# Expert layer of a streaming encoder: V rows by token, one block behind U, summed with 32-column weights

## The chip, the cores and the metric

The kernel runs on one core of one Trainium2 chip, in one launch. The metric is device time in microseconds (us), the median of three runs, from the first to the last instruction of the core. PE is the matrix engine, DVE the vector engine, ACT the scalar engine, POOL the engine that issues the indirect DMAs, SP the one that issues the plain ones.

## What is computed

One layer on 1024 prompt tokens, 32 sample tokens and 16 meta tokens of width 1024, all in fp32: a mixer (a projection, a gated linear recurrence beside a chunked matrix memory, an output projection) and then a layer of retrieved experts. The change touches the second.

```python
def block(xb):                                   # 128 tokens
    qh = (xb @ wq).reshape(PEER_BLOCK, PEER_HEADS, 2, PEER_HALF)
    s1 = jnp.einsum('thd,nd->thn', qh[:, :, 0], keys1).astype(jnp.float32)
    s2 = jnp.einsum('thd,nd->thn', qh[:, :, 1], keys2).astype(jnp.float32)
    v1, i1 = lax.top_k(s1, PEER_TOPK)
    v2, i2 = lax.top_k(s2, PEER_TOPK)
    cand = (v1[..., :, None] + v2[..., None, :]).reshape(PEER_BLOCK, PEER_HEADS, PEER_TOPK * PEER_TOPK)
    sc, ci = lax.top_k(cand, PEER_TOPK)
    e = (jnp.take_along_axis(i1, ci // PEER_TOPK, axis=-1) * PEER_KEYS
         + jnp.take_along_axis(i2, ci % PEER_TOPK, axis=-1))
    gate = jax.nn.softmax(sc, axis=-1)
    act = jax.nn.gelu(jnp.einsum('td,thkd->thk', xb, u_tab[e]).astype(jnp.float32)) * gate
    return jnp.einsum('thk,thkd->td', act.astype(xb.dtype), v_tab[e])
```

Each token picks 16 experts in each of 8 heads, 128 in all. An expert is one row of 1024 in u_tab and one in v_tab, both in HBM with 16384 rows each. The token's x is multiplied with its 128 U rows; the 128 results, through gelu and gate, weigh its 128 V rows. The sum is added to h, and a last norm gives y.

## The kernel before

The prompt is cut into 8 blocks of 128 tokens; the sample's 32 tokens are a block of their own ahead of them (b is None in the code), laid four times over the 128 partitions. The mixer of later tokens runs beside the experts of earlier ones: while block b's rows are gathered, the mixer works on block b + 1. Each engine has its program written out by hand in 128 ticks per block. In a tick, PE, DVE and ACT each do one expert's step and then what `beside` (L695, L944, L1299) puts there: the queries of a block at ticks 1 to 39 (head 0 already at tick 110 of the block before; `query` at L624, L887, L1086), the mixer at ticks 30 to 109 (`mixer` at L455, L762, L1111: projections at 37 to 78, the matrix memory from 74, the output projection at 91 to 103, the second norm at 105 to 109). All waits are counts of semaphores.

**Gathers.** The ring has eight buffers of 128 rows of 4 KB. POOL (`gathers`, L389, the DMA at L404) issues one indirect DMA per expert rank: partition p gets the row that token p has chosen as its e-th. Its order is alternating: U of tick t, V of rank t - 16; so the V rows of a head follow 16 ticks after its U rows, and the last 16 V of a block (`over`, L411) lie beside the first 16 U of the next. A gather waits until the buffer's last user is done: the dot of a U (s_dot) or the sum of a V (s_vsum). `row_of` (L241) gives the buffer and the count of arrivals. Per block: 128 U and 128 V gathers, plus 16 tiles of the query weights wq (512 KB each, two buffers) and x and y on SP's queue (`load_wq` L289, `load_x` L311, `store_y` L306).

**U side.** DVE multiplies the 128 rows with x (xcur, written by `take_over` on ACT, L910, once all dots of the last block are done) and sums along the row (`dot`, L1259; the instruction at L1266). After each head of 16, `gelu_arg` (L1268) and `coefficients` (L1281) make 16 coefficients per token, with an exponential on ACT (`gelu_exp`, L922) between them.

**V side.** ACT multiplies the identity with one coefficient column (`diagonal`, L926; all ACT instructions are recorded at L750) into one of four 128x128 buffers; PE multiplies that diagonal with the V rows, in two halves of 512 columns, and adds to acc in PSUM (`expert_sum`, L684; all matmuls are recorded at L428). A fp32 matmul is recorded as two. `take_up` (L672) first puts h into acc. At the end of a block ACT and DVE take acc out, norm it and SP stores y (`finish`, L935 and L1293). The first and the last part of the program, with fewer gathers beside the mixer, stand ahead of and behind the loops (L351, L419, L719, L977, L1336).

## Time and profile before

| what | value |
|---|---|
| median of 3 runs | 3569.66 us |
| lowest, highest run | 3557.79, 3579.22 us |
| profiled execution, first to last instruction | 3605.3 us |
| mean granted TensorE clock | 0.959 |
| instructions | 39214 |
| bytes moved | 1213.76 MB, mean 337 GB/s |
| busy: PE, DVE, ACT, POOL | 84%, 65%, 18%, 64% |

The profile gives no time of the profiled execution but its span. It is longer than each of the three timed runs, 1.0% above their median. Busy time of an engine is the union of its instructions. "Issue" as a reason for idle time means that nothing in the profile shows what was waited for. PEld is PE's weight load. The ends of matmuls are modelled, so distances between their starts are the safer reading.

### The profile page before, as it was taken

The page shows a single profiled execution, that of the slowest core. Times are in us where ns is not written, and L with a number is a line of the kernel's source. Part 1 is how long each engine was busy: PE and PEld are TensorE (multiplying, and loading weights), DVE is VectorE, ACT ScalarE, POOL GpSimd, SP SyncE. Part 2 cuts the span into 40 slices and gives each one's busy share as a digit, 9 for nine tenths or more (in the row PEclk, how much of TensorE's full clock was granted, in tenths as well). Part 3 has the DMA queues.
Part 4 walks back from the last instruction along what each step waited for, and adds up shares of the span by engine and source line. Part 5 has one row for each costly group of instructions (what it writes and reads, how often), then busy time and mean ns, then how long its engine had stood idle before and what let it go on. Part 6 is the DMA issues. An engine that isn't in the chain of part 4 may idle for free.

```text
span 3605.3 us, 39214 instructions
## 1 busy us (share of the span) xinstructions
PE 3011.3 (84%) x10724; PEld 1568.6 (44%) x10724; DVE 2354.0 (65%) x5813; ACT 658.5 (18%) x2015; POOL 2298.7 (64%) x2132
## 2 busy tenths in 40 slices
PE   7687888889987898879987798879987799877677
PEld 2553454345533454345533454345533454344222
DVE  3565975578656875578756876568655876568442
ACT  2211221112211221112211221112211121111111
POOL 0224666766777566766676567667676567667775
PEclk9799999989999999999999999999998999999999
DMA  6456989999999999999999999999999999999998
GB/s 241 161 174 240 366 316 346 371 354 351 337 372 378 348 338 351 348 361 359 330 368 357 363 314 355 361 340 369 341 353 355 364 327 345 350 375 373 355 368 296
DMA packets 340167, 1213.76 MB, mean 337 GB/s; under 512 B 41072, under 2 KB 41200, under 8 KB 339904
## 3 DMA queue, kind: packets, MB, share of 16 engines
q0 software_dynamic: 304128, 1107.43, 83.1%
q1 hardware_dynamic: 35776, 103.32, 7.7%
q8 instruction: 104, 1.70, 0.2%
q14 instruction: 159, 1.30, 0.1%
HBM read 1205.73 MB, written 4.87 MB: 336 GB/s over the span
## 4 chain that ended last, share of the span: by engine, by line
PE 37%; issue 20%; DMA 16%; DVE 9%; POOL 9%; another core or an unknown queue 6%; ACT 3%; POOLq 0%; ACTq 0%; SPq 0%; DVEq 0%
PE acc L428 23%; PE bank L428 13%; DMA ring<-peer_v,idx 11%; POOL ring L404 9%; DMA ring<-peer_u,idx 6%; DVE ring L1266 2%; ACT xn L750 1%; ACT diag L750 1%; DVE kw L1050 1%; DVE xn L1161 0%; DVE xn L1164 0%; ACT h L750 0%; ACT xT L750 0%; DVE topi L1052 0%
## 5 line engine op out<-in xcount | busy, mean ns | idle before, releaser
L428 PE MATMUL acc<-ring,diag 128*128 128x512 f32 (+1 forms) x4224 | 2086.7, 623 | 449.9 <-DMA ring<-peer_v,idx 269.1
L1266 DVE SCALAR_TENSOR_TENSOR ring<-ring,xcur 128x1024 f32<-128x1024 f32 x1056 | 1289.0, 1225 | 818.0 <-DMA ring<-peer_u,idx 744.5
L404 POOL DMA_INDIRECT ring<-peer_v,idx x1056 | 1151.2, 1090 | 643.6 <-issue 291.9
L404 POOL DMA_INDIRECT ring<-peer_u,idx x1056 | 1143.7, 1083 | 642.7 <-issue 316.5
L428 PEld LDWEIGHTS acc<-ring,diag 128*128 128x128 f32 (+1 forms) x4224 | 746.4, 192 | 1427.7 <-issue 1107.3
L750 ACT ACTIVATE diag<-ident,coef 128x128 f32<-128x128 f32 x1024 | 366.7, 395 | 646.7 <-PE acc L428 392.6
L428 PEld LDWEIGHTS bank<-xT,win 128*128 128x128 f32 (+1 forms) x2304 | 272.9, 183 | 79.2 <-issue 73.5
L428 PE MATMUL bank<-xT,win 128*128 128x128 f32 (+1 forms) x2304 | 282.6, 277 | 2.4 <-ACT xT L750 2.4
L750 ACT ACTIVATE G<-bank 128x128 f32<-128x128 f32 (+1 forms) x137 | 40.6, 296 | 830.4 <-PE bank L428 449.4
L428 PE MATMUL bank<-win,xT 128*128 128x512 f32 (+3 forms) x368 | 166.2, 583 | 1.9 <-ACT xT L750 1.9
L428 PEld LDWEIGHTS bank<-xT,qk 128*128 128x128 f32 x1024 | 131.5, 201 | 37.1 <-issue 37.1
L428 PEld LDWEIGHTS bank<-xT,t 128*128 128x128 f32 x1024 | 130.8, 200 | 36.2 <-issue 36.2
L428 PE MATMUL bank<-xT,qk 128*128 128x128 f32 x1024 | 131.3, 284 | 0.0
L428 PE MATMUL bank<-xT,t 128*128 128x128 f32 x1024 | 130.4, 283 | 0.0
L428 PEld LDWEIGHTS bank<-keysT,G 128*128 128x128 f32 x256 | 47.8, 200 | 132.9 <-issue 72.1
L428 PE MATMUL bank<-keysT,G 128*128 128x128 f32 x256 | 55.7, 301 | 57.5 <-ACT G L750 42.4
L428 PEld LDWEIGHTS bank<-win,xT 128*128 128x128 f32 (+2 forms) x368 | 60.3, 170 | 89.0 <-issue 88.7
L1266 DVE DVE_READ_ACCUMULATOR ring<-ring,xcur 128x1 f32 x1056 | 86.7, 82 | 0.0
L428 PE MATMUL bank<-wout,G 128*128 128x512 f32 (+1 forms) x144 | 70.5, 620 | 1.0 <-issue 1.0
L750 ACT ACTIVATE gl_a<-gl_a 128x16 f32<-128x16 f32 x66 | 14.0, 212 | 301.5 <-DVE gl_a L1275 154.3
L428 PE MATMUL bank<-wout,xc 128*128 128x512 f32 (+1 forms) x144 | 67.0, 593 | 0.0
L1049 DVE MAX8 tops<-bank 128x8 f32<-128x128 f32 x128 | 37.9, 296 | 31.3 <-PE bank L428 24.7
(227 smaller groups left out, 1821.1 us busy)
## 6 DMA issues: line engine op xcount, KB each, us to landing
qk<-wq SPq DMA_DIRECT2D x64, 512.0 KB
t<-wq SPq DMA_DIRECT2D x64, 512.0 KB
ring<-peer_u,idx POOLq DMA_INDIRECT x1056
ring<-peer_v,idx POOLq DMA_INDIRECT x1056
win<-w_in SPq DMA_DIRECT2D x6, 2048.0 KB, 15.1
ring<-wq SPq DMA_DIRECT2D x16, 512.0 KB, 5.1
wout<-w_out SPq DMA_DIRECT2D x1, 4096.0 KB, 22.8
xn<-x_prompt SPq DMA_DIRECT2D x8, 512.0 KB
```

The lines of the kernel that those rows point to most:

```text
L404: pool.indirect_dma_start(out=ring[:, slot, :], out_offset=None, in_=(peer_u, peer_v)[which], in_offset=bass.IndirectOffsetOnAxis(ap=idx[: ...
L428: return nc.tensor.matmul(out, lhsT, rhs, start=start, stop=stop)
L750: return nc.scalar.activation(out, in_, func, **kw)
L1049: link(dve.max(out_v[:, 0:8], values))
L1050: link(dve.match_replace(work, out_v[:, 0:8], values, -3.0e38))
L1266: stt(row, row, 1.0, xcur[:, :], ALU.mult, ALU.mult, accum_out=dots[:, column(b, e):column(b, e) + 1]).then_inc(s_dot, 1)
```

## The change

V rows are gathered by token: the partition is the expert slot (head and rank), and one DMA brings the 128 rows of one token. For that the index table is turned: DVE copies it to float, PE transposes it, ACT copies it out, DVE makes integers of it (`float_idx`, `turn_idx`, `turned_idx`). The coefficients are turned once per block by PE (`turn_coef`). A token's V sum is a matmul whose weights are 128 slots x 32 columns, all zero but one column, which holds the token's coefficients: a stripe wz with one filled column per 128 + 32, of which the matmul takes a window of 32 that puts the filled column at the token's place in its quadrant. The output is one of the four quadrants of 32 partitions of acc, and consecutive tokens go to different quadrants (`token_of`). ACT fills four tokens' columns in one copy (`token_weights`), in four sets.

The V rows of block b - 1 are gathered and summed beside the U rows of block b, eight ticks (LAG) behind. Block 0 has no V beside its U, and the V of block 7 come alone after its last U. The queries of a block begin eight ticks earlier, in `close` of the block before, where the last eight V gathers and sums lie. Gelu and coefficients are made in two groups of 64 ranks instead of eight of 16. The sum starts from a copy of h (hcur). The norm row of the second norm is no longer kept on all partitions: PE spreads it into PSUM per block. SP's stores of y move one block back. The sample keeps its scheme, with 32-column weights in wz.

```diff
 RING = 8
-DIAGS = 4
+SETS = 4
+GROUPS = 4
+LAG = 8
+HALF = 64
 QUERY_SLOTS = 5
...
-        ffn_bc = sb("ffn_bc", [P, D_MODEL])
+        ffn8 = sb("ffn8", [CM, P])
-        gl_a = sb("gl_a", [P, TOPK])
-        gl_b = sb("gl_b", [P, TOPK])
-        diag = sb("diag", [P, DIAGS, P])
+        gl_a = sb("gl_a", [P, HALF])
+        wz = sb("wz", [P, SETS * P + SAMPLE])
+        idxf = sb("idxf", [P, P])
+        idxv = sb("idxv", [P, P], u32)
+        coefT = sb("coefT", [P, P])
+        hcur = sb("hcur", [P, D_MODEL])
...
         def row_of(which, b, e):
-            turn, lead = 2 * P // RING, (2 * SAMPLE + TOPK) // RING
+            head, first, turn = 2 * SAMPLE - TOPK, (2 * SAMPLE + P) // RING, 2 * P // RING
             if b is None:
                 before, place = 0, 2 * e + TOPK + 1 if which else e if e < TOPK else 2 * e - TOPK
             elif which:
-                before, place = lead + b * turn, 2 * e + 1
-                if is_count(b, BLOCKS - 1) and e >= P - TOPK:
-                    place = e + P - TOPK
-            elif e >= TOPK:
-                before, place = lead + b * turn, 2 * e - 2 * TOPK
+                before, place = first + b * turn, 2 * e + LAG + 1 if e < P - LAG else e + P
+                if is_count(b, BLOCKS - 1):
+                    place = e
+            elif is_count(b, 0):
+                before, place = 0, head + (2 * e if e < TOPK else e + TOPK)
             else:
-                before, place = lead + (b - 1) * turn, 2 * (P - TOPK) + 2 * e
+                before, place = first + (b - 1) * turn, e if e < LAG else 2 * e - LAG
             return place % RING, (before + place // RING + 1) * 16
...
-            load_wq(0, range(10))
+            load_wq(0, range(12))
             store_y(None, y_sample)
-            with sp.Fori(0, BLOCKS - 1) as b:
+            load_x(1, x_prompt[P:2 * P, :])
+            load_wq(0, range(12, 16))
+            load_wq(1, range(10))
+            with sp.Fori(1, BLOCKS - 1) as b:
                 load_wq(b, range(10, 12))
                 load_x(b + 1, x_prompt[bass.ds(b * P + P, P), :])
                 load_wq(b, range(12, 16))
                 load_wq(b + 1, range(10))
-                store_y(b, y_prompt[bass.ds(b * P, P), :])
+                store_y(b - 1, y_prompt[bass.ds(b * P - P, P), :])
             load_wq(BLOCKS - 1, range(10, 16))
             store_states(1, BLOCKS + 1, BLOCKS)
-            store_y(BLOCKS - 1, y_prompt[(BLOCKS - 1) * P:BLOCKS * P, :])
+            for b in (BLOCKS - 2, BLOCKS - 1):
+                store_y(b, y_prompt[b * P:(b + 1) * P, :])
...
+                    if which == V and e == 0 and b is not None:
+                        pool.wait_ge(s_idxv, b + 1)
+                    if place >= RING:
+                        old, ob, oe = order[place - RING]
+                        pool.wait_ge((s_dot, s_vsum)[old], experts_before(ob) + oe + 1)
+                    elif held:
+                        for done, count in held[place]:
+                            pool.wait_ge(done, count)
+                            pool.sem_inc(s_pool_turn, 1)
                     if b is None and which == U and e == QUERY_SLOTS:
                         pool.wait_ge(s_sel, SAMPLE // TOPK)
                         pool.wait_ge(s_k_ps, 2)
                     pool.sem_inc(s_pool_turn, 1)
                     slot, _ = row_of(which, b, e)
+                    if which == V and b is not None:
+                        at = idxv[:, token_of(e):token_of(e) + 1]
+                    else:
+                        at = idx[:, column(b, e):column(b, e) + 1]
                     pool.indirect_dma_start(
                         out=ring[:, slot, :], out_offset=None, in_=(peer_u, peer_v)[which],
-                        in_offset=bass.IndirectOffsetOnAxis(ap=idx[:, column(b, e):column(b, e) + 1], axis=0)).then_inc(s_row[slot], 16)
+                        in_offset=bass.IndirectOffsetOnAxis(ap=at, axis=0)).then_inc(s_row[slot], 16)
...
-            def over(b):
-                last = (None, SAMPLE - TOPK) if is_count(b, 0) else (b - 1, P - TOPK)
-                return [x for t in range(TOPK) for x in ((U, b, t), (V, last[0], last[1] + t))]
+            def over():
+                return [x for t in range(TOPK) for x in ((U, 0, t), (V, None, SAMPLE - TOPK + t))]
+            def period(b, last):
+                both = [x for t in range(LAG, P) for x in ((U, b, t), (V, last, t - LAG))]
+                return [(U, b, t) for t in range(LAG)] + both + [(V, last, i) for i in range(P - LAG, P)]
+            def before_period(b):
+                return [((s_dot, b * P + (SAMPLE - RING + t + 1)), (s_vsum, b * P + (SAMPLE - P - LAG + t + 1))) for t in range(RING)]
             pool.wait_ge(s_qs_tile, 2 * PEER_HEADS)
             first = [(U, None, t) for t in range(TOPK)] + side_by_side(None, range(TOPK, SAMPLE))
-            gathers(first + over(0), None)
-            with pool.Fori(0, BLOCKS - 1) as b:
-                gathers(side_by_side(b, range(TOPK, P)) + over(b + 1), over(b)[-RING:])
+            gathers(first + over() + [(U, 0, t) for t in range(TOPK, P)], None)
+            with pool.Fori(1, BLOCKS - 1) as b:
+                gathers(period(b, b - 1), before_period(b))
             b = BLOCKS - 1
-            gathers(side_by_side(b, range(TOPK, P)) + [(V, b, j) for j in range(P - TOPK, P)], over(b)[-RING:])
+            gathers(period(b, b - 1) + [(V, b, i) for i in range(P)], before_period(b))
...
+                if tick == T_NORM2 + 1:
+                    if is_count(v, 0):
+                        pe.wait_ge(s_rows_bc, 32)
+                    pe.wait_ge(s_h2, w + 1)
+                    for c in range(CM):
+                        last = mm(by4(bank[c // 4])[0:n, c % 4, :], spread(ident[0:CM, c:c + 1], 1, n), ffn8[:, :])
+                    last.then_inc(s_ffn_ps, 1)
...
-            def expert_sum(b, j):
-                n = n_experts(b)
-                slot, arrived = row_of(1, b, j)
+            def sample_sum(j):
+                slot, arrived = row_of(1, None, j)
                 pe.wait_ge(s_row[slot], arrived)
-                pe.wait_ge(s_diag, experts_before(b) + j + 1)
+                pe.wait_ge(s_wz, j + 1)
                 for half in range(2):
-                    last = mm(acc[0:n, 512 * half:512 * half + 512], diag[:, j % DIAGS, 0:n],
-                              ring[:, slot, 512 * half:512 * half + 512], start=False, stop=j == n - 1)
+                    last = mm(acc[0:SAMPLE, 512 * half:512 * half + 512], wz[:, P * (j % SETS):P * (j % SETS) + SAMPLE],
+                              ring[:, slot, 512 * half:512 * half + 512], start=False, stop=j == SAMPLE - 1)
                 last.then_inc(s_vsum, 1)
-            def beside(b, tick, more):
+            def token_sum(b, i):
+                m, g = divmod(i, GROUPS)
+                slot, arrived = row_of(1, b, i)
+                if g == 0:
+                    pe.wait_ge(s_wz, sets_before(b) + m + 1)
+                pe.wait_ge(s_row[slot], arrived)
+                at = P * (m % SETS) + SAMPLE * (g + 1) - 1 - m
+                for half in range(2):
+                    last = mm(acc[SAMPLE * g:SAMPLE * g + SAMPLE, 512 * half:512 * half + 512], wz[:, at:at + SAMPLE],
+                              ring[:, slot, 512 * half:512 * half + 512], start=False, stop=m == P // GROUPS - 1)
+                last.then_inc(s_vsum, 1)
...
+            def close(b, last, more):
+                for k in range(LAG):
+                    if last is not None:
+                        token_sum(last, P - LAG + k)
+                    if more:
+                        queries(b + 1, k - LAG)
+                    if k == LAG - 2:
+                        turn_coef(b, more)
+                take_up(b)
...
+            def token_weights(b, m):
+                if m == 0 and is_count(b, 0):
+                    act.wait_ge(s_wz0, 1)
+                elif m == 0:
+                    act.wait_ge(s_ct, b + 1)
+                act.wait_ge(s_vsum, experts_before(b) + GROUPS * (m - SETS + 1))
+                to = wz[:, P * (m % SETS):P * (m % SETS) + P].rearrange("p (g c) -> p g c", g=GROUPS)[:, :, SAMPLE - 1]
+                a(to, coefT[:, :].rearrange("p (g m) -> p g m", g=GROUPS)[:, :, m], ACT.Copy).then_inc(s_wz, 1)
...
+                pe.wait_ge(s_coef, groups_before(b) + 2)
+                pe.wait_ge(s_topk, heads_before(b) + PEER_HEADS + (1 if more else 0))
+                nc.tensor.transpose(bB[:, 0:P], coef[:, :], ident[:, :]).then_inc(s_ct_ps, 1)
...
+            def close(b, last, more):
+                gelu_exp(b, 1)
+                if more:
+                    take_over(b + 1)
+                    for k in range(LAG):
+                        queries(b + 1, k - LAG)
+                turned_coef(b)
+                if last is not None:
+                    finish(last)
...
             def gelu_arg(b, g):
-                first = column(b, TOPK * g)
-                d = dots[:, first:first + TOPK]
-                dve.wait_ge(s_dot, experts_before(b) + TOPK * g + TOPK)
...
+                link(tt(c, d, gate[:, first:first + width], ALU.mult))
...
             def coefficients(b, g):
-                dve.wait_ge(s_gexp, heads_before(b) + g + 1)
-                link(ts(gl_a[:, :], gl_a[:, :], 1.0, None, ALU.add))
-                link(dve.reciprocal(gl_a[:, :], gl_a[:, :]))
-                tt(coef[:, column(b, TOPK * g):column(b, TOPK * g) + TOPK], gl_a[:, :], gl_b[:, :], ALU.mult).then_inc(s_coef, 1)
-            def dots_of(b, e):
-                dot(b, e)
+                width = TOPK if b is None else HALF
+                first = column(b, width * g)
+                c, x = coef[:, first:first + width], gl_a[:, 0:width]
+                dve.wait_ge(s_gexp, groups_before(b) + g + 1)
+                link(ts(x, x, 1.0, None, ALU.add))
+                link(dve.reciprocal(x, x))
+                tt(c, c, x, ALU.mult).then_inc(s_coef, 1)
...
+            def turned_idx(b):
+                dve.wait_ge(s_itf, b + 1)
+                if not is_count(b, 0):
+                    dve.wait_ge(s_vsum, experts_before(b))
+                dve.tensor_copy(idxv[:, :], idxf[:, :]).then_inc(s_idxv, 1)
...
+            def close(b, last, more):
+                gelu_arg(b, 1)
+                for k in range(LAG):
+                    if k == 1:
+                        coefficients(b, 1)
+                    if more:
+                        queries(b + 1, k - LAG)
+                if last is not None:
+                    finish(last)
+                turned_idx(b)
```

## Rows read from the trace of the kernel before

**Rows 1.** The page: busy shares of the engines, and the DMA digits by slice.

```profile
PE 3011.3 (84%) x10724; PEld 1568.6 (44%) x10724; DVE 2354.0 (65%) x5813; ACT 658.5 (18%) x2015; POOL 2298.7 (64%) x2132
...
DMA  6456989999999999999999999999999999999998
```

**Rows 2.** Stretches: from:to and length, busy us, clock, DMA share, GB/s.

```profile
1182.00:1592.00 410.00, 350.04 (x1252) 187.03 (x1252) 281.24 (x688) 76.14 (x235) 278.21 (x256) 0.97 0.95 351
...
3315.00:3565.00 250.00, 170.61 (x336) 58.53 (x336) 112.58 (x216) 32.95 (x88) 188.98 (x169) 0.98 0.96 354
1280.00:1400.00 120.00, 116.55 (x484) 67.16 (x483) 83.24 (x159) 23.83 (x72) 83.75 (x79) 1.00 0.94 339
1210.00:1250.00 40.00, 33.43 (x130) 18.98 (x131) 37.03 (x120) 9.69 (x30) 24.80 (x24) 0.96 1.02 406
...
3570.00:3588.00 18.00, 17.78 (x42) 7.90 (x42) 0.00 (x0) 4.90 (x14) 10.36 (x12) 1.00 0.98 366
```

**Rows 3.** Instruction groups of 1182:1592: busy us, mean ns | idle before, releasers.

```profile
L428 PE MATMUL acc<-ring,diag 128*128 128x512 f32 x512 | 251.2, 620 | 50.6 <-DMA ring<-peer_v,idx 31.6 <-ACT diag L750 13.5 <-issue 5.3
L1266 DVE SCALAR_TENSOR_TENSOR ring<-ring,xcur 128x1024 f32<-128x1024 f32 x128 | 156.4, 1225 | 94.5 <-DMA ring<-peer_u,idx 85.8 <-issue 7.3
L404 POOL DMA_INDIRECT ring<-peer_u,idx x128 | 141.0, 1102 | 52.3 <-issue 40.4 <-PE acc L428 10.4 <-DVE ring L1266 1.5
L404 POOL DMA_INDIRECT ring<-peer_v,idx x128 | 137.4, 1074 | 79.7 <-issue 33.4 <-PE acc L428 22.6 <-DVE ring L1266 12.0
...
L750 ACT ACTIVATE diag<-ident,coef 128x128 f32<-128x128 f32 x128 | 45.4, 395 | 63.8 <-PE acc L428 38.2 <-issue 17.5 <-remote 4.6
```

**Rows 4.** ACT's copies into xcur (start, us); dots: ns min/median/max, first and last start.

```profile
311.26 1.06 ACT L750 ACTIVATE xcur<-xn 128x1024 f32<-128x1024 f32 x1 [3.73 <-DVE ring L1266]
...
719.97 1.06 ACT L750 ACTIVATE xcur<-xn 128x1024 f32<-128x1024 f32 x1 [7.82 <-DVE ring L1266]
...
3178.72 1.06 ACT L750 ACTIVATE xcur<-xn 128x1024 f32<-128x1024 f32 x1 [8.33 <-issue]
...
L1266 DVE SCALAR_TENSOR_TENSOR ring<-ring,xcur x1056: 1160/1225/1300, 160.6 to 3566.7; 128x1024 f32<-128x1024 f32 x176
```

**Rows 5.** PE in order of time: start us, us; 32-column weights, then 128.

```profile
196.69 1.90 PE L428 MATMUL acc<-ring,diag 128*32 128x512 f32 x4
198.53 5.62 PE L428 MATMUL bank<-xT,win 128*128 128x128 f32 x48
...
1320.36 1.95 PE L428 MATMUL bank<-xT,win 128*128 128x128 f32 x16
1322.14 1.88 PE L428 MATMUL acc<-ring,diag 128*128 128x512 f32 x4
1323.86 0.38 PE L428 MATMUL bank<-xT,win 128*128 128x128 f32 x2
```

**Rows 6.** PE's records on acc in half us, sample queries: busy (x records).

```profile
110.00:110.50 0.50, 0.50 (x7) 1.00 0.89 229
110.50:111.00 0.50, 0.50 (x10) 1.00 0.83 344
...
111.50:112.00 0.50, 0.50 (x7) 1.00 0.88 336
```

**Rows 7.** One of the small gelu operations, whole run: busy us, mean ns.

```profile
L1273 DVE TENSOR_SCALAR gl_a<-gl_a 128x16 f32<-128x16 f32 x66 | 11.5, 175 | 2.3
```

**Rows 8.** The end, in order of time: PE, POOL, then ACT, DVE.

```profile
3570.42 27.70 PE L428 MATMUL acc<-ring,diag 128*128 128x512 f32 x64 [0.22 <-issue]
...
3571.56 0.94 POOL L404 DMA_INDIRECT ring<-peer_v,idx  x1 [0.30 <-issue]
...
3598.16 1.02 ACT L750 ACTIVATE xn<-acc 128x1024 f32<-128x1024 f32 x1 [6.46 <-PE acc L428]
...
3600.79 1.28 DVE L1297 SCALAR_TENSOR_TENSOR xn<-xn,stat,final_bc 128x1024 f32<-128x1024 f32 x1 [30.95 <-ACT stat L750]
```

**Rows 9.** One piece of the chain that ended last: start us, us, from issue to landing.

```profile
3317.33 5.33 DMA ring<-peer_v,idx
```

More of the change, by code:

```diff
@@ L52 @@
 T_QUERY0 = 110
+T_HCUR = 3
+T_IDXF, T_IDX = 60, 95
 T_MIXER = T_NORM
@@ L641, in query @@
                         pe.wait_ge(s_topk, heads_before(b) + head - 1)
+                    if ft == 5 and not is_count(b, 0):
+                        pe.wait_ge(s_ct, b)
                     pe.wait_ge(s_q2, b * 16 + ft + 1)
@@ L697, in beside @@
                 for head in range(1, PEER_HEADS):
                     query(b, head, tick - T_QUERY - QUERY_TICKS * (head - 1))
+            def beside(b, tick, more):
+                queries(b, tick)
                 if more:
@@ L701, in beside, with period @@
                     query(b + 1, 0, tick - T_QUERY0)
+                if tick == T_IDX:
+                    turn_idx(b)
+            def period(b, last, more):
+                for tick in range(P):
+                    if tick >= LAG:
+                        token_sum(last, tick - LAG)
+                    beside(b, tick, more)
+            def close(b, last, more):
[7 more added lines that the diff above has]
+                take_up(b)
             for tick in range(T_MIXER, BLOCK_TICKS):
@@ L942, in finish, with queries, beside @@
                 rstd(n, 6, D_MODEL).then_inc(s_rstd_y, 1)
-            def beside(b, tick, more):
+            def queries(b, tick):
                 for head in range(1, PEER_HEADS):
                     query(b, head, tick - T_QUERY - QUERY_TICKS * (head - 1))
+            def beside(b, tick, more):
+                queries(b, tick)
                 if more:
@@ L949, in beside, with period @@
                     query(b + 1, 0, tick - T_QUERY0)
+                if tick == HALF + 1:
+                    gelu_exp(b, 0)
+                if tick == T_IDX + 1:
+                    act.wait_ge(s_it_ps, b + 1)
+                    a(idxf[:, :], bF[:, 0:P], ACT.Copy).then_inc(s_itf, 1)
+            def period(b, last, more):
+                for tick in range(P):
+                    if tick % GROUPS == 2:
+                        token_weights(last, tick // GROUPS)
+                    if tick == T_HCUR:
+                        keep_h(b)
+                    beside(b, tick, more)
+            def close(b, last, more):
[7 more added lines that the diff above has]
+                    finish(last)
             nc.scalar.preload_act_table_set("natural_log_exp_and_others")
-            act.wait_ge(s_const, 7)
+            act.wait_ge(s_const, 6)
             act.wait_ge(s_setup_a, 1)
@@ L1287, in dots_of @@
-            def dots_of(b, e):
-                dot(b, e)
+                width = TOPK if b is None else HALF
+                heads = width // TOPK
+                first = column(b, width * g)
+                d, c, x = dots[:, first:first + width], coef[:, first:first + width], gl_a[:, 0:width]
+                dve.wait_ge(s_dot, experts_before(b) + width * (g + 1))
+                link(tt(x, d, d, ALU.mult))
+                link(ts(x, x, GELU_CUBIC, 1.0, ALU.mult, ALU.add))
+                link(tt(x, x, d, ALU.mult))
```

241 lines of the change are left out of this document (133 added, 108 removed).

## The prediction

> **What bounds the kernel now.** I began with the page [rows 1]: PE is busy 84% of the span, DVE 65%, POOL 64%, and the DMA digit stands at 8 or 9 from the fourth slice on. So I read next one period, the 410 us between two hand-overs of a block [rows 2] (1182:1592). It moves 351 GB/s at a DMA share of 0.95: 256 gathers of 128 rows of 4 KB (0.524 MB each), 16 tiles of wq and 1 MB of x and y. The 250 us in which nothing but gathers and sums ran [rows 2] (3315:3565) move 354 GB/s at 0.96 with PE at 68% and DVE at 45%. One gather per 0.524/354 = 1.48 us is thus what this ring of eight reaches without any crowd on the engines. With PE full, in the projections, it is 339 GB/s [rows 2] (1280:1400), and beside the query weights, which come by SP's queue, 406 GB/s in all [rows 2] (1210:1250).
>
> Then I asked who holds the gathers back. In the period POOL issues 256 of them in 278 us and sits idle 132 us more [rows 3]. About 0.30 us of idle stand between any two issues [rows 8], 77 us in all; the other 55 us are waits for a free slot of the ring, 33 us of them named after PE's sums and 13.5 after DVE's dots. PE waits 31.6 us for V rows and 13.5 us for ACT's diagonals; DVE waits 85.8 us for U rows [rows 3]. The gathers are the bound, first by their own rate, then by V slots that PE frees late.
>
> **The change, part by part.** Every number is set against the profiled span, 3605.3 us. That execution is 1.0% above the median of the three runs (3569.66 us); I carry the difference in us over to the median. Starting points: the hand-overs of x (the copy into xcur) are at 311.3, 720.0, ... 3178.7, so six and more periods of 409.6 us on average ((3178.7 - 311.3)/7), and the last dot ends at 3568, 389 us after the last hand-over and 37 us before the end [rows 4]. Up to 311 nothing of weight changes.
>
> *Block 0 without V.* The first period now gathers U alone, 128 gathers instead of 256. By gathers it would need 128 x 1.48 = 189 us and 16 tiles of wq. DVE doesn't let it: it is the engine with the most left to do. Its period is 410 us less the 85.8 us that it waits for U rows [rows 3] = 324. I take 8 off for the gelu (below) and add 2 for the index copies and the split multiplication by the norm row: 318 us, so -91 against 409. PE, which loses 251 us of sums in it, is out of the way. Lower end: DVE's waits for the other engines shrink too, 295. Upper end: the chains of the mixer, spread over 3.2 us ticks before, no longer fit under 2.4 us ticks, 340.
>
> *The V sums of a period.* A token still streams 2 halves of 512 columns in 4 records. A record takes 0.43 us with 128 columns of weights (1322.14 to 1323.86 are four) and no less with 32 (196.69 to 198.53: 1.84 us, 0.12 more) [rows 5]. Changing between the shapes costs PE time: the 48 projection records after it take 5.62 us where three runs of 16 at 1.78 (1320.36 to 1322.14) and a drain of 0.17 make 5.51 [rows 5]. So 0.12 + 0.11, I take 0.25 us per token beside which PE projects; some 65 ticks have such work: 16 us more of PE time in each period. Against it stands overlap. In the sample's queries the output quadrant changes every 32 records; just there ten records lie in half a us and otherwise seven [rows 6], so the new quadrant's records start while the old ones still stream. Consecutive tokens go to different quadrants. A token that finds PE behind, with its row landed and no projection between, can overlap the one before, up to 1.72 us. In a run of seven projection ticks three pairs stand together: in backlog 5.2 us saved against 1 us lost. [...]
>
> *Diagonals.* 128 ACT copies of 395 ns go, 45 us of ACT per period, and with them PE's 13.5 us of waiting for them [rows 3]; 32 strided copies of 4 columns, six ticks ahead, take their place. ACT was not the bound; only what PE frees earlier counts.
>
> *Gelu.* Eight groups of 11 small operations at about 0.2 us become two on 64 columns: 18 us to at most 6 us of DVE [rows 7], 12 less, 8 after the waits on ACT. Where DVE already waits for rows this gives nothing.
>
> *The close of a block.* After dot 127 DVE runs gelu, one and a half heads of queries, the last block's norm and the turned indices before its next dot: some 20 us. Meanwhile POOL has the last 8 V and 8 U of the next block, 16 x 1.48 = 24 us, then must wait for the turned indices and for dot 0. The queue runs dry for 3 to 6 us. The old crossing had its own wait of 8 us of POOL. I set the difference at 0, bounds -3 and +8.
>
> *Steady period.* Bounds: above 410, as now, and +8 for the close; below, 256 x 1.48 = 379 with no wait for slots at all, and wq in its shadow, which nothing in the trace does over a whole period; I put the end at 390 since DVE is at 93% in the query stretch [rows 2] (1210:1250). I take 402. The 120 us of projections going from 339 to 354 GB/s give 5 us, and of the 13.5 us for diagonals I count 3, as most of the rest is hidden in the same lateness. It is near the upper end because most V slots are late through projections, which stay. Six periods: -48. The last, without a mixer, -3.
>
> *The end.* Before, 37 us followed the last dot. Now: the last 8 V of block 6, 8 x 1.48 = 12; the sum of the last (2), ACT's two passes and the root (3600.79 - 3598.16 = 2.6), DVE's 1.28 and the copy of the indices (0.2) before the first V of block 7 may be issued; 5.3 us from issue to landing [rows 8, 9]: 24 us. Then 127 gathers of V alone. POOL's floor is 1.24 us each [rows 8], PE's 27.70/16 = 1.73 where sums don't overlap [rows 8]; the old V-only end ran at 366 GB/s, 1.43 us [rows 2] (3570:3588). I take 1.45 (overlap holds): 184. The last sum 2 and the finish 7: 217 in all, +180.
>
> Nothing else is on the path. The norm row by PE (8 small matmuls) runs beside ACT's square of the same 1024 columns, 1.02 us [rows 8]; ACT, 18% busy [rows 1], has room for the copy of h. SP stores y a block later and loads x behind that store as before, with most of a period to spare; if that cover failed, the mixer would start late by one transfer, some 5 us per block.
>
> Sum: -91 - 48 - 3 + 180 = +38. 3605 becomes 3643; the median 3569.66 becomes **3608 us**. Within this forecast the first period (295 to 340), the steady ones (398 to 406) and the tail (1.40 to 1.50) leave 3575 to 3645.
>
> **Rivals.**
> 1. *PE was the brake of the V slots and it is gone*: of the 55 us of slot waits a third goes, 18 us, every period takes 392, and block 0 takes 308. For it: most idle of POOL stands before V gathers (79.7 against 52.3) [rows 3]. Against it: the quiet 250 us reach only 354 GB/s. Six times -10 and -10, -10 for the seventh: -80 against my sum, 3528 us. Faster than before.
> 2. *The mode changes weigh more than the overlap*: in the mixed stretch no pair overlaps, 16 us of PE time go straight into the 200 us where PE is the bound, less 8 for the diagonals, periods of 418; and V alone runs at 1.73. Six times +16, and 127 x 0.28 = 36: +132, 3740 us. It decides from the point where the mean of PE's work per tick passes 2.9 us, the pace of two gathers.
> 3. *Periods stay at 410*: the change only moves work to both ends. 8 x 6 = 48 more, 3656 us. For it: the DMA share is 0.95 in crowded and in quiet stretches alike.
> 4. *V rows of one token come at another rate* than rows of one rank, since they share the first key; no row shows it. It would move the tail and the periods either way and lies inside 1 and 2.
>
> **Chances.** Forecast 40%, rival 1 20%, rival 2 13%, rival 3 27%. A measurement of this kernel tells some 0.5% (18 us) from no change. Faster: most of rival 1 and a sliver of mine, 0.20. Same: a third of mine and the edge of rival 1, 0.17. Slower: the rest, 0.63. The range runs from below rival 1 to above rival 3: 3510 to 3700 us, leaving out rival 2 and the tail of rival 1.
>
> **What would show it.** Hand-over 0 to 1 near 318 us with DVE over 85% busy and DMA near 0.65; later hand-overs 402 us apart; no wait of PE for ACT in the sums; about 9.5 us between sets of four V sums in quiet stretches and more than ten records in half a us where PE catches up; 190 us or less between the first and last sum of block 7, at 360 GB/s. Wrong if the steady periods differ from 402 by over 8, if block 0 takes under 295, or if the tail runs at PE's 1.73.

## The result, and the profile after

The changed kernel takes 3656.81 us (median of 5 runs, 3652.75 to 3675.40), against 3572.36 us for the kernel before beside it: ratio 1.025, 95% interval 1.0208 to 1.0292. A repeat beside the kernel before gave 3674.72 against 3566.56, ratio 1.0295 (1.0249 to 1.0342). Forecast was 3608, 1.1% slower or +38 us. Measured is +84 us between the medians: slower, as forecast, and inside the range of 3510 to 3700 us, but by more than twice as much.

The page of the changed kernel, where [rows 1] stand for the kernel before:

```profile
PE 2982.5 (81%) x10884; PEld 1214.2 (33%) x10884; DVE 2288.0 (62%) x5425; ACT 357.9 (10%) x1223; POOL 2297.6 (63%) x2131
...
PEclk9798777999999999999989999999999998999999
DMA  6456878999999998999999898999999998999898
```

The hand-overs of x in the changed kernel, in order of time (start us, us), against [rows 4]:

```profile
317.43 1.06 ACT L849 ACTIVATE xcur<-xn 128x1024 f32<-128x1024 f32 x1 [3.72 <-DVE ring L1407]
...
612.85 1.04 ACT L849 ACTIVATE xcur<-xn 128x1024 f32<-128x1024 f32 x1
...
3063.28 1.04 ACT L849 ACTIVATE xcur<-xn 128x1024 f32<-128x1024 f32 x1
```

Its dots (ns min/median/max, first and last start):

```profile
L1407 DVE SCALAR_TENSOR_TENSOR ring<-ring,xcur x1056: 1148/1224/1292, 164.4 to 3455.4; 128x1024 f32<-128x1024 f32 x176
```

These marks split the two profiled spans, 3605.3 and 3673.5 us:

| stretch | before | after | difference | forecast |
|---|---|---|---|---|
| start to hand-over 0 | 311.3 | 317.4 | +6 | 0 |
| block 0 | 408.7 | 295.4 | -113 | -91 |
| six periods (hand-over 1 to 7) | 2458.7 | 2450.4 | -8 | -48 |
| block 7, to its last dot's start | 388.0 | 392.1 | +4 | -3 |
| last dot's start to the end | 38.6 | 218.1 | +180 | +180 |
| sum | 3605.3 | 3673.5 | +68 | +38 |

The first row is scatter: in eleven other profiles of this kernel and its variants it lies between 311 and 318. Block 0 and the end came about as priced or better. The six periods hardly shrank: 408.4 us each, against 409.8 before and 402 forecast. Even these 8 us lie in the first of the six (395 us against 405); in the other five the periods are as long as before (411.1 against 410.8, from dot 127 to dot 127). The profiled executions are 68 us apart, the medians 84: 16 us of the slowdown stand in no row of this table.

The view of stretches (from:to and length, busy us of PE, PEld, DVE, ACT and POOL, granted clock, DMA share, GB/s) of the changed kernel: block 0; then one period cut at its dots 127, 40, 88, 127; then the V rows alone.

```profile
320.00:612.00 292.00, 164.44 (x820) 112.81 (x819) 267.59 (x634) 36.10 (x115) 181.45 (x146) 0.77 0.84 295
1415.70:1562.50 146.80, 116.88 (x447) 50.09 (x445) 112.56 (x339) 18.18 (x62) 89.07 (x83) 0.94 0.92 344
1562.50:1708.80 146.30, 138.65 (x573) 61.38 (x572) 100.95 (x182) 14.63 (x49) 105.80 (x98) 1.00 0.96 348
1708.80:1822.50 113.70, 94.55 (x252) 27.25 (x253) 60.08 (x119) 6.21 (x24) 80.78 (x78) 0.98 0.98 374
...
3480.00:3655.00 175.00, 169.10 (x483) 43.36 (x484) 0.00 (x0) 5.89 (x28) 113.16 (x122) 0.99 0.97 362
```

And the same three parts of a period of the kernel before:

```profile
1535.90:1675.80 139.90, 114.86 (x461) 66.72 (x462) 114.97 (x356) 29.09 (x94) 89.11 (x85) 0.96 0.97 367
1675.80:1825.70 149.90, 139.00 (x557) 78.54 (x555) 103.63 (x198) 29.13 (x87) 102.98 (x96) 0.99 0.93 334
1825.70:1941.20 115.50, 93.90 (x235) 40.41 (x236) 63.05 (x137) 18.12 (x53) 81.60 (x78) 0.97 0.98 370
```

In the first part, from the last dot of a block to dot 40 of the next, the DMA share fell from 0.97 to 0.92 and the rate from 367 to 344 GB/s; it is longer by 7 us in this period, 4.7 in the mean of five. In the second and third the rate rose and they are a little shorter (0.6 and 3.8 us in the mean). So about half of the gain forecast for the projections and the diagonals was there, nearly all of it behind the projections, and the crossing from block to block ate it. Where, DVE shows (start us, us, idle time before it in brackets; the small operations of gelu and of head 1's choices are left out):

```profile
1415.72 1.23 DVE L1407 SCALAR_TENSOR_TENSOR ring<-ring,xcur 128x1024 f32<-128x1024 f32 x1 [2.00 <-DMA ring<-peer_u,idx]
...
1425.79 0.30 DVE L1191 MAX8 tops<-bank 128x8 f32<-128x128 f32 x1 [5.93 <-PE bank L469]
...
1431.86 0.30 DVE L1191 MAX8 tops<-bank 128x8 f32<-128x128 f32 x1 [4.38 <-PE bank L469]
...
1440.13 1.28 DVE L1447 SCALAR_TENSOR_TENSOR xn<-xn,stat,final_bc 128x1024 f32<-128x1024 f32 x1 [3.46 <-ACT stat L849]
1441.34 0.22 DVE L1459 CAST idxv<-idxf 128x128 uint32<-128x128 f32 x1
1446.06 1.23 DVE L1407 SCALAR_TENSOR_TENSOR ring<-ring,xcur 128x1024 f32<-128x1024 f32 x1 [4.50 <-issue]
```

Thirty us between two dots: two waits for head 1's scores, one for the norm, and 4.50 us in which the profile shows nothing, at the turn of DVE's loop over blocks. POOL in the same place:

```profile
1438.37 0.94 POOL L437 DMA_INDIRECT ring<-peer_u,idx  x1 [1.43 <-issue]
1448.10 1.09 POOL L437 DMA_INDIRECT ring<-peer_u,idx  x1 [8.79 <-DVE ring L1407]
1450.90 0.94 POOL L437 DMA_INDIRECT ring<-peer_v,idxv  x1 [1.72 <-DVE ring L1407]
1453.51 0.94 POOL L437 DMA_INDIRECT ring<-peer_u,idx  x1 [1.67 <-DVE ring L1407]
1456.37 0.94 POOL L437 DMA_INDIRECT ring<-peer_v,idxv  x1 [1.93 <-DVE ring L1407]
...
1471.52 0.94 POOL L437 DMA_INDIRECT ring<-peer_u,idx  x1 [2.02 <-DVE ring L1407]
```

The ring (the eight buffers that all gathers share) holds eight U rows and nothing else. The wait of 8.79 us was expected in kind. What was not: each of the next eight gathers, U or V, waits for one dot, and a dot beside a choice comes only every 2.9 us. These eight gathers take 23.4 us (1448.10 to 1471.52), where the queue at 1.48 us each would need 12.

### The profile page after: what moved, and what is told of

It is laid out like the page before. It is cut to its first block, busy times and chain, and to the rows that moved or that the text cites. A ratio compares the mean times of both kernels' runs of the same rounds, so it can differ in the third digit from the quotient of the medians.

```text
span 3673.5 us, 37305 instructions
## 1 busy us (share of the span) xinstructions
PE 2982.5 (81%) x10884; PEld 1214.2 (33%) x10884; DVE 2288.0 (62%) x5425; ACT 357.9 (10%) x1223; POOL 2297.6 (63%) x2131
## 4 chain that ended last, share of the span: by engine, by line
PE 32%; issue 20%; DVE 18%; DMA 16%; POOL 8%; another core or an unknown queue 3%; ACT 1%; POOLq 0%; DVEq 0%; SPq 0%; ACTq 0%
PE acc L469 20%; DMA ring<-peer_v,idxv 13%; PE bank L469 12%; POOL ring L437 8%; DVE ring L1407 6%; DMA ring<-peer_u,idx 3%; DVE kw L1192 1%; DVE kw L1202 1%; DVE eh L1203 1%; DVE kw L1200 1%; DVE topi L1194 1%; ACT xn L849 1%; DVE tops L1193 1%; DVE topi L1195 1%
## 5 line engine op out<-in xcount | busy, mean ns | idle before, releaser
L469 PE MATMUL acc<-ring,wz 128*32 128x512 f32 x4224 | 1892.2, 617 | 386.7 <-DMA ring<-peer_v,idxv 341.9
L437 POOL DMA_INDIRECT ring<-peer_u,idx x1056 | 1125.6, 1066 | 781.8 <-issue 448.6
L437 POOL DMA_INDIRECT ring<-peer_v,idxv x1024 | 1135.0, 1108 | 544.9 <-issue 281.0
L469 PEld LDWEIGHTS acc<-ring,wz 128*32 128x32 f32 x4224 | 376.9, 111 | 1577.8 <-issue 871.3
L469 PE MATMUL bank<-xT,win 128*128 128x128 f32 (+1 forms) x2304 | 292.7, 283 | 5.8 <-issue 3.3
L469 PE MATMUL bank<-xT,qk 128*128 128x128 f32 x1024 | 142.9, 297 | 22.8 <-DMA qk<-wq 20.7
L469 PE MATMUL bank<-xT,t 128*128 128x128 f32 x1024 | 141.3, 295 | 23.8 <-issue 19.2
L1447 DVE SCALAR_TENSOR_TENSOR xn<-xn,stat,final_bc 128x1024 f32<-128x1024 f32 (+1 forms) x9 | 11.6, 1284 | 231.3 <-ACT stat L849 229.0
L469 PE MATMUL bank<-keysT,G 128*128 128x128 f32 x256 | 66.3, 343 | 92.4 <-ACT G L849 84.7
L849 ACT ACTIVATE wz<-coefT 128x4 f32<-128x4 f32 x256 | 49.7, 206 | 470.7 <-PE acc L469 293.1
```

What stands on the lines that cost most here:

```text
L437: pool.indirect_dma_start(out=ring[:, slot, :], out_offset=None, in_=(peer_u, peer_v)[which], in_offset=bass.IndirectOffsetOnAxis(ap=at, a ...
L469: return nc.tensor.matmul(out, lhsT, rhs, start=start, stop=stop)
L849: return nc.scalar.activation(out, in_, func, **kw)
```

## Experiments

For every kernel the starts of its 1024 prompt dots were taken from the trace and averaged over blocks 2 to 6 (the first column is from dot 127 of the block before to dot 0; "V alone" is the time from first to last gather of block 7's V, over 127):

```
                         127-0   0-8  8-40  40-88 88-127  period  V alone
before                     3.2  26.8 112.4  150.6  117.8   410.8     -
after                     30.1  23.4  93.5  150.0  114.0   411.1   1.438
after, repeated           30.3  23.4  92.9  151.3  112.8   410.7   1.438
e1 late close             22.3  28.6  93.4  152.3  115.4   412.1
e2 queries at tick 1      24.2  15.8  97.6  148.2  113.3   399.2
e10 queries at tick -3    27.5  22.3  94.1  150.2  112.9   406.9
e9 e2 and late close      14.8  21.8 100.9  147.5  113.5   398.5   1.426
e3 same quadrant          31.4  23.4  93.5  154.6  113.2   416.2   1.640
e8 wide weights           30.1  23.4  93.1  150.6  114.3   411.5   1.679
e4 rows of a rank         29.9  23.4  93.8  152.2  112.7   412.0   1.444
e5 half sums              28.8  23.4  94.0  147.3  114.1   407.7   1.398
e7 half sums and dots     32.1  19.2  91.5  149.9  112.5   405.3   1.403
e11 e9 without loops      14.2  20.3 100.4  146.6  114.0   395.5
e12 before without loops   3.5  26.4 105.5  150.8  115.7   401.8
```

Two executions of the changed kernel differ by up to 1.3 us in a column. e3, e4, e5, e7, e8, e2 and e10 were timed once each.

**e1, the close itself.** In DVE's program:

```diff
+                if more:
+                    period(b + 1, True, range(DOTS_FIRST))
+                turned_idx(b)
                 if last is not None:
                     finish(last)
-                turned_idx(b)
```

and the loop starts at tick 2 (DOTS_FIRST is 2).

> From the changed kernel, where dot 0 of a block starts 30.1 us after dot 127 of the block before (mean of blocks 2 to 6) and a period takes 411.1 us. Here DVE does dots 0 and 1 of the next block, and turns the indices, before the last norm, and takes its loop turn (4.5 us without an instruction) behind them. Theory A (the close eats the gain: POOL waits for dot 0 with a dry queue): dot 0 comes 21 to 24 us after dot 127, the period is 403 to 407 us, and the whole kernel 30 to 55 us faster than the changed one. Rival B (the gathers' own rate sets the period, and what is lost in the close is made up later): dot 0 is earlier as well, but the period stays within 2 us of 411 and the whole within 12 us.

Dot 0 came 7.8 us earlier, as expected, but ranks 0 to 8 took 5.2 us more, since the loop turn and the norm now lie there, and the period is 412.1. 3668.83 us (ratio to before 1.0174, 1.0115 to 1.0232), 5 us under e4, whose stretches are the changed kernel's, on the same chip. These are rival B's numbers. Theory A falls in this form: moving the gap doesn't remove it.

**e2, the queries back at tick 1.**

```diff
-T_QUERY = 1 - LAG
+T_QUERY = 1
...
                 if last is not None:
+                    act.wait_ge(s_xcur, streams_before(b) + (2 if more else 1))
                     finish(last)
```

> The queries begin at tick 1 again, so that the close holds none of head 1's choices. Theory A: the stretch without dots falls from 30 to 20 us or less, but the queries then reach 8 ticks further into the block, where DVE is 93% busy; ranks 0 to 40 take 7 to 10 us more than 117, so that the period is 408 to 413 us. Theory C (the earlier queries are themselves the loss): the period falls to 404 us or less. Rival B: 411 within 2 us.

3597.27 us in one run, 76.6 under e4 (one run too) on the same chip; before stood at 3612.30 there (3582.27 to 3617.69). The period is 399.2: theory C's number. The edit is the tick and a wait of ACT for its own copy of x. The stretch without dots shrank by only 6 us, though; ranks 0 to 8 gave 7.6, and ranks 8 to 40, where the moved choices now lie, took back 4.1. DVE's busy time from dot 127 to dot 40 is the same (112.4 against 112.6 us, means of the same blocks). POOL of e2 at the crossing:

```profile
1422.22 0.94 POOL L437 DMA_INDIRECT ring<-peer_u,idx  x1 [0.30 <-issue]
1430.12 1.14 POOL L437 DMA_INDIRECT ring<-peer_u,idx  x1 [6.95 <-DVE ring L1408]
1431.56 1.99 POOL L437 DMA_INDIRECT ring<-peer_v,idxv  x1 [0.30 <-issue]
1433.86 1.99 POOL L437 DMA_INDIRECT ring<-peer_u,idx  x1 [0.30 <-issue]
1436.15 0.94 POOL L437 DMA_INDIRECT ring<-peer_v,idxv  x1 [0.30 <-issue]
...
1445.91 1.08 POOL L437 DMA_INDIRECT ring<-peer_u,idx  x1 [2.76 <-PE acc L469]
```

DVE finds eight landed U rows and no choice to make beside the first ones; its dots run back to back, and behind the same kind of wait (6.95 us) eight gathers take 15.8 us (1430.12 to 1445.91) instead of 23.4. Its first part of a period, against 0.92 and 344 GB/s above:

```profile
1401.90:1541.60 139.70, 115.18 (x457) 50.98 (x456) 112.52 (x339) 18.51 (x62) 92.63 (x85) 0.99 0.95 363
```

That made theory D: what costs is the stretch from dot 127 to dot 8, in which only dots free slots.

**e10, queries at tick -3.**

```diff
-T_QUERY = 1 - LAG
+T_QUERY = -3
```

ACT's wait is in it as in e2. It tells D from the wait inside the close: here no choice of DVE lies in the close, but seven lie beside dots 0 to 7.

> Queries from tick -3: PE and ACT still have part of head 1's work in the close, but DVE's first choice of head 1 falls beside dot 1, so seven choice steps lie beside dots 0 to 7, against eight in the changed kernel and three or four in e2. Theory D (a dot beside a choice takes 2.9 us and frees one slot, so ranks 0 to 8 are slow by the number of choices beside them): ranks 0 to 8 take 21 to 23 us, the period is 404 to 409 us. Rival C (it is the wait of DVE inside the close, for scores that PE makes between V sums): the period falls to e2's 399 or below, since no choice is left there.

22.3 us and a period of 406.9; 3633.72 us in one run. Both as D says, and C as this expectation puts it (the wait inside the close is all of it), 399 or below, falls. The wait has a part, though: of the 4.2 us that the period lost, 2.6 are in the stretch without dots and 1.1 in ranks 0 to 8. Between ticks -7, -3 and 1 the period goes 411, 407, 399.

**e9, both edits.** e2, and in DVE's close:

```diff
+                if more:
+                    period(b + 1, True, range(1))
+                turned_idx(b)
+                if more:
+                    period(b + 1, True, range(1, DOTS_FIRST))
                 if last is not None:
                     finish(last)
-                turned_idx(b)
```

(DOTS_FIRST is 3.)

> Queries from tick 1 (as e2) and, in DVE's order, dot 0 of the next block, then the turned indices, dots 1 and 2, and only then the last norm and the loop turn. Theory D (what costs is the stretch from dot 127 to dot 8, in which eight lone U rows fill the ring and only dots free slots; it took 53.5 us for 21.4 gathers in the changed kernel and 40.0 for 21 in e2): dot 0 comes at 16 to 19 us, dot 8 at 31 to 36 us after dot 127, the period is 391 to 396 us against e2's 399.2, and the whole kernel 30 to 50 us below e2's 3597, thus 1 to 3% below the kernel before. Rival B (the gathers' own rate, 1.47 us, makes up for whatever the close loses): within 3 us of 399.

Dots 0 and 8 came at 14.8 and 36.6 us, nearly as D expected, but ranks 8 to 40 took 3.3 us more than e2's, and the period, 398.5, is rival B's: the second edit brought nothing that these runs can tell (e2's one run was 0.996 of the kernel before on its own chip). From dot 127 to dot 40 the DMA share is now that of the kernel before:

```profile
1398.00:1535.40 137.40, 114.12 (x453) 51.73 (x452) 113.00 (x340) 18.52 (x62) 89.29 (x84) 0.96 0.97 369
```

84 gathers and the wq tiles fill it. 3571.45 us in 10 runs, 103 under the changed kernel beside it (3674.72), and 1.0005 (0.9982 to 1.0028) of the kernel before: the slowdown is gone, and no more.

**e3 and e8, overlap and shape changes.** e3 gives consecutive tokens to one quadrant (its sums and `token_weights` take their places from i accordingly); e8 uses all 128 columns of a set as weights and writes all of acc, so that neither quadrants nor shape changes are left. First e3's edit, then e8's:

```diff
-            return SAMPLE * (i % GROUPS) + i // GROUPS
+            return i
```

```diff
-                    last = mm(acc[SAMPLE * g:SAMPLE * g + SAMPLE, 512 * half:512 * half + 512], wz[:, at:at + SAMPLE],
+                    last = mm(acc[:, 512 * half:512 * half + 512], wz[:, at:at + P],
```

> Consecutive tokens go to the same quadrant of 32 partitions, so their matmuls can't overlap; the four columns of a set lie in one block of coefT. If the overlap is what kept PE out of the way: the 128 gathers of V alone at the end go from 1.44 to about 1.7 us each (+35 us), and ranks 40 to 88, beside the projections, from 150 to 156 to 160 us. If the gathers' rate hides PE (rival B): the end still becomes slower since 1.73 us of PE per sum is over 1.44, but ranks 40 to 88 stay within 2 us of 150. If matmuls of different quadrants don't overlap in these sums at all: nothing changes, 1.44 and 150.

> From the changed kernel; the V sums use 128 columns of weights and write 128 partitions, as before the change (each row is then added with four tokens' coefficients: that part of the output is another computation). Neither shape changes nor overlap are left. e3 (no overlap, shape changes) took 5.5 us more per period and 1.64 us per gather of V alone. If the shape change costs 0.25 us at each of some 65 ticks and PE were the bound there, this gives back up to 8 us of e3's loss beside the projections: ranks 40 to 88 at 147 to 151 us, V alone at 1.62 to 1.73 us. If the gathers hide the shape changes: ranks 40 to 88 at 153 to 156, as e3.

e3 took 3738.21 us and e8 3718.93, one run each on different chips. Without overlap ranks 40 to 88 take 3.3 to 4.6 us more (154.6; the expectation had 156 to 160, or within 2 us of 150); without the shape changes as well, 4.0 of them come back (150.6, within the 147 to 151 expected). So the two, both real, cancel beside the projections. V alone needs the overlap: 1.64 and 1.68 us per gather against 1.44. The PE rows of the changed kernel show both, first a sum and 16 records of a projection, then sums alone:

```profile
1628.70 1.91 PE L469 MATMUL acc<-ring,wz 128*32 128x512 f32 x4 [0.31 <-DMA ring<-peer_v,idxv]
1630.53 2.05 PE L469 MATMUL bank<-xT,win 128*128 128x128 f32 x16
1632.51 1.90 PE L469 MATMUL acc<-ring,wz 128*32 128x512 f32 x4
...
3559.61 10.62 PE L469 MATMUL acc<-ring,wz 128*32 128x512 f32 x32
```

A pair takes 1632.51 - 1628.70 = 3.81 us; in [rows 5] it took 3.50 (1320.36 to 1323.86), which is the short end there. Over all such pairs from 800 us on without idle time between them, the median is 3.82 us of 54 here and 3.60 of 62 in the kernel before: 0.22 us for the two changes of shape. e8, without them, has 3.60 again. Eight sums take 10.62 us, 1.33 each, against 1.73 in [rows 8]; most other sums of this stretch wait for rows. So the trace shows both: sums in different quadrants overlap, 0.40 us for each of these eight, and the two changes of shape cost 0.22 us of PE time.

The view of groups in the stretch of V alone (busy us, mean ns | idle us before it and releasers) shows whom POOL waits for, in the changed kernel and in e8:

```profile
L437 POOL DMA_INDIRECT ring<-peer_v,idxv x128 | 119.9, 937 | 76.7 <-issue 32.8 <-PE acc L469 30.9 <-DVE idxv L1459 13.0
```

```profile
L437 POOL DMA_INDIRECT ring<-peer_v,idxv x128 | 119.9, 937 | 105.9 <-PE acc L469 71.3 <-issue 22.9 <-DVE idxv L1459 11.7
```

**e4, another index.**

```diff
-                        at = idxv[:, token_of(e):token_of(e) + 1]
+                        at = idx[:, e:e + 1]
```

> The V gathers read a column of the index table that isn't turned: 128 tokens' rows of one rank in each gather, as in the kernel before. The sums are then of the wrong rows (the V gather is changed, nothing else). If rows of one token come at another rate than rows of one rank (rival 4 of the prediction), the 128 gathers of V alone change from 1.438 us each by over 3%, and the periods with them. If not, all stay within 1%: 1.42 to 1.45 us, periods 409 to 413.

3673.83 us in one run. 1.444 against 1.438 us, periods 412.0 against 411.1: rows of one token come at the rate of rows of one rank. Rival 4 is out.

**e5 and e7, less work per row.**

```diff
-                for half in range(2):
+                for half in range(2 if m == P // GROUPS - 1 else 1):
```

and in e7 also, in the dots of the prompt's blocks:

```diff
-                stt(row, row, 1.0, xcur[:, :], ALU.mult, ...
+                if b is not None:
+                    row = row[:, 0:512]
+                stt(row, row, 1.0, xcur[:, 0:512 if b is not None else D_MODEL], ALU.mult, ...
```

> From the changed kernel; each V row's sum takes only the first 512 columns (the second half of y's expert sum is left out but for the last token of each quadrant), so PE is relieved of some 110 us per period; gathers are whole. Theory B (beside the projections the gathers' rate is the bound): ranks 40 to 88 keep 147 to 150 us and ranks 88 to 127 stay at 112 to 114. If PE still is the brake there (V slots come free late): ranks 40 to 88 fall to 138 to 143 us. In the close the last V sum comes 1 us earlier, no more; the 128 gathers of V alone stay at 1.42 to 1.45 us each.

> From the changed kernel; each dot takes 512 of 1024 columns and each V sum too (half of the expert layer's arithmetic is left out, no gather is). DVE is relieved by some 0.5 us at each dot. Theory D (from dot 127 to dot 40 DVE's work sets the time): ranks 0 to 8 take 19 to 20 us, and dot 127 to dot 40 falls from 147 to 134 to 140 us. Rival B: what DVE gains is lost again at the queue, so that dot 127 to dot 40 keeps 144 us or more. Ranks 40 to 127 stay at 258 to 262 us, as with the half sums alone (261.4), since there only gathers count.

e5 took 3644.26 us and e7 3608.64, one run each on different chips. Half the sums bring ranks 40 to 88 to 147.3 us, the lower edge of what B said: 2.7 to 4 us less than with whole ones, where a PE that is the brake would have given 7 or more. V alone went to 1.398 us per gather, just below the expected 1.42. The stretches of e5, in the parts used above, show a second effect:

```profile
1409.50:1555.60 146.10, 104.06 (x373) 49.44 (x374) 112.70 (x340) 18.20 (x62) 88.39 (x81) 0.77 0.92 344
1555.60:1704.70 149.10, 117.17 (x477) 56.75 (x477) 100.78 (x182) 14.55 (x49) 109.47 (x98) 0.87 0.94 340
1704.70:1820.20 115.50, 84.25 (x175) 23.60 (x173) 59.93 (x120) 6.21 (x24) 82.80 (x77) 0.72 0.97 368
```

PE is idle more, and the granted clock falls from 0.94, 1.00 and 0.98 to 0.77, 0.87 and 0.72, so it is not a clean halving of PE's time: in the second part PE's busy time fell by 21.5 us (138.65 to 117.17), where 48 sums of 0.86 us less are 41. With the dots halved too, ranks 0 to 8 fell to 19.2 us as expected, but dot 127 to dot 40 took 142.8 us, between what D (134 to 140) and B (144) said: DVE then idles 28.6 us in ranks 8 to 40, 17 of them for U rows, where it idles 14.3 in the changed kernel. So the evidence is for D where the queue is dry, and for B behind it.

**e11 and e12, no loops.** The loops over blocks written out on all engines, in e9 and in the kernel before:

```diff
-            with pool.Fori(1, BLOCKS - 1) as b:
+            for b in turns(1, BLOCKS - 1):
```

> e9 with the loops over blocks written out on all engines, so that no engine takes a loop turn (4.2 to 4.5 us without an instruction on PE and DVE at each crossing). If the turns lie on the path: dot 127 to dot 40 falls from 137.5 to 132 to 135 us, the period from 398.5 to 393 to 396, the whole by 20 to 40 us to some 3535 to 3550. If the rows' rate in that stretch is the bound (83 gathers and 16 tiles of wq in 137.5 us), or the longer program costs as much in fetching: within 8 us of e9's 3571.

> The kernel before with its loops over blocks written out. There POOL's turn leaves the queue 8 us without an issue and ranks 8 to 16 take 34.7 us where others take 25 to 27. If the turn is on the path: ranks 8 to 16 at 28 to 31 us, the period 404 to 408 instead of 410.8, and the whole 0.5 to 1.3% below the kernel before. If not: within 0.3%.

e12 takes 3542.51 us against 3600.32, ratio 0.985 (0.9816 to 0.9885), more than expected: ranks 8 to 16 fell from 34.7 to 30.4 us, the period by 9. POOL's turn in the kernel before, in front of the gather of U row 16, and the same gather without a loop:

```profile
1579.88 0.94 POOL L404 DMA_INDIRECT ring<-peer_v,idx  x1 [0.30 <-issue]
1588.78 0.94 POOL L404 DMA_INDIRECT ring<-peer_u,idx  x1 [7.96 <-PE acc L428]
```

```profile
1556.31 0.94 POOL L418 DMA_INDIRECT ring<-peer_v,idx  x1 [0.31 <-issue]
1557.55 1.80 POOL L418 DMA_INDIRECT ring<-peer_u,idx  x1 [0.30 <-issue]
```

The 7.96 us are named after PE, but PE is not their cause: this gather takes the slot of U row 12, whose dot (started at 1577.55) was over by 1578.8, and the indices of head 1 stood at 1571.6. All six turns back of the kernel before have such a gap, 7.08 to 8.17 us; in e12 0.30 or 0.31 us stand there.

e11 gives 3578.49 against 3600.32 on the same chip, 0.9945 (0.992 to 0.997), where e9 had 1.0005 on another: 0.6%, with the period 3 us shorter, the low end of what was expected. The best version found is e12, the old scheme without loops; no form of the changed scheme that was timed more than once beat it.

## Why the prediction was off

- **Block 0 without V**: -113 for -91. That DVE would set it was right (267.6 us busy of 292). 295 was my lower end; it counted on DVE's waits for ACT and PE to shrink, the forecast did not. The DMA share was 0.84, where I had said near 0.65.
- **The end**: 218 us, forecast 217 and 0.6 for the last dot. V alone at 1.438 for 1.45; e3 and e8 show that without the overlap it would have been some 26 to 31 us more.
- **Steady period, the failed step.** I had -8 (410 to 402): -5 for the projections, -3 for the diagonals, 0 for the close. Measured over blocks 2 to 6: -0.6 in ranks 40 to 88, -3.8 in ranks 88 to 127, and **+4.7 from dot 127 to dot 40** (142.4 to 147.1); together +0.3, where I had said that over 8 from 402 is wrong. Two terms failed, by about as much: the projections' -5, taken up below, and the close, "I set the difference at 0, bounds -3 and +8". The +4.7 lies within these bounds, but its cause was not in my account. I counted some 20 us without dots and a dry queue of 3 to 6 us; it was 30.1 us, and I stopped at dot 0. Eight lone U rows in the ring mean that the next eight gathers each cost a dot, and the queries, begun eight ticks earlier, put a choice beside each. I listed that move and never priced it. Put back (e2) it is worth 12 us a period, and the forecast's 402 is then beaten.
- **Projections**: the mechanism was misjudged, not only its size. The shape changes were priced about right (0.22 us in the median for 0.25); the overlap is 0.40 us per sum (1.73 to 1.33) where I allowed up to 1.72 per pair, and beside the projections the two cancel. With half the sums, which took PE's busy time there from 138.65 to 117.17 us, those ranks give only 3 to 4 us. So PE's work reaches this stretch only in small part, and nothing was left of my 5 us.
- **Diagonals**: ranks 88 to 127, which hold few projections, gave 3.8 us for my 3. No run takes the diagonals away alone; that it is they is argued, not shown.
- **Rivals.** Rival 1 (PE frees the slots, periods 392) is wrong, rival 2 (418, 1.73 per V; its mode changes are the changes of shape) too: e3 (416.2, 1.64) comes close to it, which says what the quadrants are worth. Rival 3, periods of 410, gave 3656 us, within 1 us of the median. That closeness is luck: its periods came out by a cancellation (+4.7 against -4.4), while its block 0 was 22 us too long and 16 us of the measured slowdown stand in no row of the table. I gave it 27% against 40% for my own.
- **Signs.** PE no longer waits for ACT in the sums of a steady period, and V alone came at 362 GB/s with 182.6 us from first to last gather, as said. Two signs were wrong in themselves: four V sums go with eight gathers, 11.4 us apart in the quiet 3200 to 3450 us and not 9.5, and where sums overlap three or four records lie in half a us, not over ten.

## What to carry to other kernels

With a shared ring of buffers, ask at each seam of the schedule which consumer can free the next slot; if the ring is full of one kind, the whole queue runs at that consumer's pace, and work put beside it there costs more than the same work elsewhere (here 12 us a period). Price every step that a change moves, at the place where it arrives. And price the turn of a large loop from a trace (here 2.33 to 4.26 us of PE, 2.93 to 4.50 of DVE, 7.08 to 8.17 of POOL), and look at what the queue does meanwhile.

## What the runs showed of the hardware

- In the two profiles of the changed kernel each of the five turns back of the loop over blocks leaves DVE 2.93 to 4.50 us and PE 2.33 to 4.26 us without an instruction, with nothing in the profile waited for; entering and leaving the loop leave DVE 0.21 and 0.00 us. POOL's six turns back in the kernel before leave 7.08 to 8.17 us. In e12, where the loops are written out on all engines, 0.30 or 0.31 us stand there, and the kernel before is 1.5% faster (3542.51 against 3600.32 us). What an engine does in such a gap no run shows.
- Halving PE's sums (e5) lowered the granted clock of the three stretches of a period from 0.94, 1.00 and 0.98 to 0.77, 0.87 and 0.72, and part of the relief was lost with it: in e5, 16 records of a projection took 3.78 us at 1603.07 us, at a granted clock of 0.50, and 2.05 at 1611.08, at 1.00. The mean clock of the whole execution was 0.806 in e5 and 0.811 in e7, against 0.941 in the changed kernel.
- The median of the kernel before was 3566.56 to 3612.30 us in the four sets of runs, 1.3% apart: whole times are compared only with what ran beside them.
